# Weight chunks split in halves with the row block outermost, the modulation product in plain fp32 from the raw chunk and placed around the norms, and the small projection first in its layer

## The reference, cut to what matters

```
h = rms_norm(x, norm_w[layer]); proj = h @ w_in[layer]                  # first block, per layer
(a_xbc, a_z, a_dt, b_q, b_k, b_v, b_z, c_q, c_k, c_v, c_f, c_z, gates) = split(proj)
x = x + sum_i(sigmoid(gate_i) * (y_i @ w_proj[layer, i])) @ w_out[layer]

m = silu(cond) @ w_mod[l] + b_mod[l]         # 2 x 1024 @ 1024 x 6144: shift, scale, gate, twice
h = rms_norm(x, norm_mix[l]) * (1 + scale1) + shift1                    # second block, per layer
x = x + gate1 * (merge(attention, pool, fourier of h @ w_in[l]) @ w_out[l])
h = rms_norm(x, norm_ffn[l]) * (1 + scale2) + shift2
x = x + gate2 * ((val * silu(gate)) @ w_down[l])                        # val, gate: conv of h @ w_up[l]
```

## Time and profile before

| | |
|---|---|
| runs | 2406.66, 2407.77, 2414.5 us; median 2407.77 |
| profiled execution | 2407.12 us; span 2405.3 us |
| TensorE busy | 2173.5 us of the span, mean granted clock 0.953 |
| VectorE, ScalarE, GpSimd busy | 1444.4, 1160.4, 697.9 us |
| moved | 330.66 MB, 137 GB/s over the span |

### The profile page before, as it was taken

The page is one execution under the profiler, slowest core; times in us unless marked ns, Lnnn a source line. Parts: engine busy times, 40 slices in busy tenths (PEclk is TensorE's granted clock), DMA queues, the critical chain, the costliest instruction groups (busy, mean ns, idle before and its releaser), DMA issues.

```text
span 2405.3 us, 35434 instructions
## 1 busy us (share of the span) xinstructions
PE 2173.5 (90%) x14868; PEld 1926.8 (80%) x14868; DVE 1444.4 (60%) x1930; ACT 1160.4 (48%) x1688; POOL 697.9 (29%) x208
## 2 busy tenths in 40 slices
PE   5998979997898989996999998989999969998997
PEld 5888879997788889985867776667778858797996
DVE  5677856555676756565267336565554655845675
ACT  4575474544575475544266333444333344645543
POOL 0222333342322423352101132454441112122331
PEclk9999999998899999996999999999999979998999
DMA  5544434545444435552111234334332212253552
GB/s 202 186 164 153 166 106 158 210 176 183 158 159 158 143 120 177 193 193 97 45 45 48 101 114 147 125 140 175 141 140 105 89 56 84 88 193 113 196 182 70
DMA packets 51982, 330.66 MB, mean 137 GB/s; under 512 B 5488, under 2 KB 8688, under 8 KB 14832
## 3 DMA queue, kind: packets, MB, share of 16 engines
q1 hardware_dynamic: 51824, 328.41, 37.9%
HBM read 327.21 MB, written 1.18 MB: 137 GB/s over the span
## 4 chain that ended last, share of the span: by engine, by line
PE 67%; DVE 18%; ACT 11%; issue 3%; POOL 1%; DMA 1%; SPq 0%; ACTq 0%; DVEq 0%
PE ps L731 18%; PE ps L732 18%; PE ps L733 18%; ACT t_hi L1068 5%; DVE t_lo L1378 3%; DVE t_SQA L1388 2%; DVE t_A L1821 2%; PE ps L776 1%; PE ps L744 1%; PE ps L745 1%; PE ps L746 1%; PE ps L777 1%; PE ps L987 1%; PE ps L847 1%; DVE t_A L1806 1%
## 5 line engine op out<-in xcount | busy, mean ns | idle before, releaser
L731 PE MATMUL ps<-t_RB,t_hi 128*128 128x256 f32 (+1 forms) x3712 | 1176.8, 317 | 54.0 <-DVE t_MOD L1431 11.9
L732 PE MATMUL ps<-t_RB,t_hi 128*128 128x256 f32 (+1 forms) x3712 | 1158.2, 312 | 0.0
L733 PE MATMUL ps<-t_RB,t_lo 128*128 128x256 f32 (+1 forms) x3712 | 1156.8, 312 | 0.0
L1847 POOL TENSOR_TENSOR t_lo<-t_raw,t_hi 128x2048 fp32r<-128x2048 f32 (+2 forms) x140 | 619.0, 4424 | 1424.4 <-ACT t_hi L1068 1397.7
L1068 ACT ACTIVATE t_hi<-t_raw 128x2048 fp32r<-128x2048 f32 (+2 forms) x316 | 571.0, 1809 | 769.3 <-PE ps L733 700.4
L731 PEld LDWEIGHTS ps<-t_RB,t_hi 128*128 128x128 f32 x3712 | 720.6, 194 | 125.1 <-issue 22.8
L733 PEld LDWEIGHTS ps<-t_RB,t_lo 128*128 128x128 f32 x3712 | 720.6, 194 | 35.9
L732 PEld LDWEIGHTS ps<-t_RB,t_hi 128*128 128x128 f32 x3712 | 721.3, 194 | 34.6 <-issue 1.2
L1378 DVE TENSOR_TENSOR t_lo<-t_raw,t_hi 128x2048 fp32r<-128x2048 f32 (+2 forms) x176 | 418.3, 2378 | 459.7 <-ACT t_hi L1068 454.1
L1806 DVE SCALAR_TENSOR_TENSOR t_A<-ps,t_V,t_A 128x510 f32<-128x510 f32 (+1 forms) x176 | 102.0, 611 | 119.2 <-ACT t_A L1338 117.6
L744 PE MATMUL ps<-t_hi,t_RB 128*128 128x256 f32 (+1 forms) x320 | 96.5, 302 | 15.8 <-DVE t_RB L1665 10.3
(11 more groups left out here) (304 smaller groups left out, 2205.8 us busy)
## 6 DMA issues: line engine op xcount, KB each, us to landing
t_raw<-in_W SPq DMA_DIRECT2D x286, 1024.0 KB, 4.8
t_raw<-in_W SPq DMA_DIRECT2D x14, 512.0 KB, 3.7
t_A<-cu_scratch SPq DMA_DIRECT2D x8, 512.0 KB, 5.1
t_B<-cu_scratch SPq DMA_DIRECT2D x8, 512.0 KB, 5.8
t_raw<-in_W SPq DMA_DIRECT2D x16, 256.0 KB, 3.0
t_A<-in_C SPq DMA_DIRECT2D x2, 1536.0 KB, 8.2
t_X<-in_X SPq DMA_DIRECT2D x2, 512.0 KB, 4.1
t_X<-in_X SPq DMA_DIRECT2D x1, 1024.0 KB, 7.4
```

The lines of the kernel that those rows point to most:

```text
L731: mm(o, hi[:, k, w], xh(k), start=k == 0, stop=False)
L732: mm(o, hi[:, k, w], xl(k), start=False, stop=False)
L733: i = mm(o, lo[:, k, w], xh(k), start=False, stop=k == nkt - 1)
L1847: tt(t.lo[s][:, 0:w], t.raw[r][:, 0:w], t.hi[s][:, 0:w].bitcast(F), ALU.subtract).then_inc(*up("pool", ("split", u.i)))
```

## The change

1. A chunk wider than 1024 elements is split in two halves of four row blocks. The first half's `lo` is always GpSimd's; the second is GpSimd's for odd chunks where `share` is set, and VectorE's otherwise. `chan` and `toks` take the row block outermost and the column blocks or token blocks inside. The event `used` exists per half. In the list of units GpSimd gets 368 parts and VectorE 138, where they had 140 and 176 splits, most of them twice as wide.
2. The modulation isn't split. `mod` multiplies `raw` in plain fp32 with 32 stationary columns (`C32`, 2 used, the others 0), row block k into the partitions 32 (k mod 4) on: 8 matmuls. ScalarE copies 128 x 256 to `MT`, and `mod2` adds the four partial sums up and turns them by two matmuls with a constant (`sel`), into a bank of the side work's ring. A modulation row holds its `raw` buffer until TensorE has used it.
3. Modulation units come every twelve gemms in block 1 and every three in most of block 2, and `rstd(t, fill)` puts up to two ahead of the sum of squares, one between it and the spreading matmul (now the unit `rstdb`) and one behind: (2, 1, 1) at t = 1, 3 and 4, (2, 1, 0) at t = 2; the last unit stands just ahead of t = 5. So 16 of the 48 units stand at norms and 32 among the gemms.
4. `small(l)` comes first in its layer, with a tick of its own and one empty step ahead of `small4`. `squares(8)` starts after the last `k` gemm.
5. Block 2's attention mask is stored in 768 columns, not 1024.

```diff
 
+    def turn_mod(self):
+
+        if self.open:
+            l, c = self.open
+            self.add("mod2", l=l, c=c, s=(self.sbank(),))
...
@@ -218,30 +227,32 @@
     def some_mods(self, n):
         for _ in range(n):
             if self.mods:
-                l, c = self.mods.pop(0)
-                i = self.chunk("mod", CH, wcols("w_mod_2", l, np.arange(c * 256, c * 256 + 256)))
-                self.split_after(i)
-                self.add("mod", l=l, c=c, i=i, g=(self.bank(),))
-
-                def turned(l=l, c=c):
-                    self.add("mod2", l=l, c=c, g=(self.bank(),))
-                    return
-                    yield
-                self.side.append(turned())
+                self.turn_mod()
+                l, c = self.open = self.mods.pop(0)
+                self.add("mod", l=l, c=c, g=(self.bank(),))
+
+    def need_mods(self, l, j):
+
+        while self.mods and self.mods[0] < (l, 4 * j + 4):
+            self.some_mods(1)
+        if self.open and self.open < (l, 4 * j + 4):
+            self.turn_mod()
 
...
-        i = self.chunk("split", nkt * ncol, fn)
+        i = self.chunk(nkt * ncol, fn)
         nm, per = ncol // 128, 512 // tw
         for m0 in range(0, nm, per):
             last = m0 + per >= nm
             if last and not urgent:
-                self.split_after(i)
+                self.split_after(i, 0)
             n = then(m0) if then else ()
             self.add(kind, l=l, c=c, i=i, g=(self.bank(),), n=n, x=(m0, min(nm, m0 + per), *x))
             if last and urgent:
                 self.drain()
-                self.split_after(i)
+                self.split_after(i, 0)
+            if last:
+                self.split_after(i, 1)
             if self.fine and not last:
                 self.tick()
...
+        self.small(l)
         qk(0)
-        if l == 1:
-            self.side.append(self.squares(8))
-        self.small(l)
         self.vproj(l, "vc", O_VC, 4)
...
+        if l == 1:
+            self.side.append(self.squares(8))
...
+    def rstd(self, t, fill):
+
+        self.some_mods(fill[0])
+        self.add("rstd", l=t, g=(self.bank(),))
+        self.some_mods(fill[1])
+        b = (self.bank(),)
+        self.add("rstdb", l=t, g=b)
+        self.some_mods(fill[2])
+        return b
+
     def plain(self, t):
-        b = (self.bank(), self.bank())
-        self.add("rstd", l=t, g=b)
+        b = self.rstd(t, (2, 1, 0))
...
+    rows = [u for u in units if u.kind == "mod" or u.kind == "split" and u.c == 0]
 
     def load(j):
-        w = widths[j]
+
+        if j >= len(rows):
+            return
+        if j >= NR:
+            old = rows[j - NR]
+            q.wait_ge(at("split", old.i) if old.kind == "split" else at("modmm", old.l, old.c))
+        w = rows[j].x[0]
         e.dma_start(t.raw[j % NR][:, 0:w], t.d["W"][j, :, 0:w]).then_inc(*up(f"w{j % NR}", ("raw", j), by=16))
...
-        if u.kind == "split" and u.i + NR < n:
-            q.wait_ge(at("split", u.i))
-            load(u.i + NR)
+        if u.kind == "mod" or u.kind == "split" and u.x[3]:
+            load(u.x[1] + NR)
...
     def chan(u, nkt, ncol, tw, xh, xl, point, *events):
 
         hi, lo = weights(u, nkt, ncol)
         b = gbank(u)
-        for j, m in enumerate(range(u.x[0], u.x[1])):
-            o, w = b[:, j * tw:(j + 1) * tw], slice(m * 128, m * 128 + 128)
-            for k in range(nkt):
-                q.wait_ge(point(k))
-                mm(o, hi[:, k, w], xh(k), start=k == 0, stop=False)
+        for k in range(nkt):
+            q.wait_ge(point(k), at("split", u.i, k * ncol // 1024))
+            for j, m in enumerate(range(u.x[0], u.x[1])):
+                o, w = b[:, j * tw:(j + 1) * tw], slice(m * 128, m * 128 + 128)
+                mm(o, hi[:, k, w], xh(k), start=k == 0 and j == 0, stop=False)
                 mm(o, hi[:, k, w], xl(k), start=False, stop=False)
-                i = mm(o, lo[:, k, w], xh(k), start=False, stop=k == nkt - 1)
-        i.then_inc(*up("pe", ("mm", u.i, u.x[0]), ("used", u.i), *events))
+                i = mm(o, lo[:, k, w], xh(k), start=False, stop=k == nkt - 1 and m == u.x[1] - 1)
+            taken(u, i, k, nkt, ncol)
+        ended(u, i, nkt * ncol, ("mm", u.i, u.x[0]), *events)
...
     def mod(u):
-        q.wait_ge(at("split", u.i), at("cond"))
-        s = u.i % NS
-        hi, lo = (p[s][:, :].rearrange("p (k c) -> p k c", k=8) for p in (t.hi, t.lo))
+
+        q.wait_ge(at("raw", u.x[1]), at("cond"))
+        w = t.raw[u.x[1] % NR][:, :].rearrange("p (k c) -> p k c", k=8)
         b = gbank(u)
         for k in range(8):
-            c = t.C4[:, k, :, :].rearrange("p q c -> p (q c)")
-            mm(b[0:4, 0:256], c, hi[:, k, :], start=k == 0, stop=False)
-            i = mm(b[0:4, 0:256], c, lo[:, k, :], start=False, stop=k == 7)
-        i.then_inc(*up("pe", ("mm", u.i, 0), ("used", u.i)))
+            j = k % 4
+            i = mm(b[32 * j:32 * j + 32, 0:256], t.C32[:, k, :], w[:, k, :], start=k < 4, stop=k >= 4)
+        i.then_inc(*up("pe", ("modmm", u.l, u.c)))
 
     def mod2(u):
+
         q.wait_ge(at("mt", u.l, u.c))
-        b = gbank(u)
+        b = sbank(u)
         for m in range(2):
-            i = e.transpose(b[:, 4 * m:4 * m + 4], t.MT[:, m * 128:(m + 1) * 128], t.ident[0:4, 0:4])
+            i = mm(b[:, 2 * m:2 * m + 2], t.MT[:, m * 128:(m + 1) * 128], t.vec("sel", 0, 2), start=True, stop=True)
         i.then_inc(*up("pe", ("modt", u.l, u.c), ("mtr", u.l * 24 + u.c)))
...
     def split(u):
-        s, r, w = u.i % NS, u.i % NR, u.x[2]
-        q.wait_ge(at("raw", u.i), was("used", u.i - NS))
-        act(t.hi[s][:, 0:w], t.raw[r][:, 0:w], ACT.Copy).then_inc(*up("act", ("hi", u.i), ("split", u.i)))
+        s, r, w = u.i % NS, u.x[1] % NR, slice(1024 * u.c, min(u.x[0], 1024 * u.c + 1024))
+        q.wait_ge(at("raw", u.x[1]), was("used", u.i - NS, u.c))
+        act(t.hi[s][:, w], t.raw[r][:, w], ACT.Copy).then_inc(
+            *up("act", ("hi", u.i, u.c), ("split", u.i, u.c), ("split", u.i)))
...
-            kind, w, _ = o.chunks[u.i]
-            u.x = ("pool" if kind == "mod" or (u.x[0] and u.i % 5 in (1, 3)) else "dve", kind, w)
+            w, fn = o.chunks[u.i]
+            if u.c == 0:
+                rows.append((w, fn))
+                row[u.i] = len(rows) - 1
+            elif w <= 1024:
+                continue
+            u.x = (w, row[u.i], "pool" if u.c == 0 or u.x[0] and u.i % 2 else "dve", u.c == 1 or w <= 1024)
+        elif u.kind == "mod":
+            u.x = (CH, len(rows))
+            rows.append((CH, wcols("w_mod_2", u.l, np.arange(u.c * 256, u.c * 256 + 256))))
         units.append(u)
-    return units, o.chunks
+    return units, rows
 
 
 def build(nc, units, d):
```

More of the change, by code:

```diff
@@ L526, in whole @@
         for i in range(NS):
-            self.add("split", i=i, x=(False,))
-        self.every = 6
+            for half in range(2):
+                self.add("split", i=i, c=half, x=(False,))
+        self.every = 12
         self.layer1(0)
@@ L1889, in plan @@
     o = Order().whole()
-    units = []
+    units, rows, row = [], [], {}
     for u in o.units:
```

171 lines of the change are left out of this document (92 added, 79 removed).

## The result

| | before | after |
|---|---|---|
| median of the runs, us | 2409.93 (2406.66 to 2414.5, 4 runs) | 2322.97 (2320.64 to 2326.04, 4 runs) |
| profiled execution, us | 2407.12 | 2326.04; span 2324.3, mean granted clock 0.956 |

The ratio is 0.9639, with a 95% interval of 0.9616 to 0.9661: 3.6% faster, 87 us. The forecast was 2332, in a range of 2296 to 2385.

What follows compares the result with a forecast made beforehand. The prediction took TensorE's stream, broken by short chains on other engines, as the bound. Terms -46 + 21.5 - 15 - 17 - 14.5 - 5 = -76 us from 2407.1, plus 0.65 for the median, gave 2332 us, range 2296 to 2385.

Steps and rivals of the forecast that it cites:

- Modulation's matmuls: On TensorE, 48 units costing 100 us become 32 units among the gemms costing 54 us: -46 us.
- the waits that go: TensorE's gemm waits behind `mod2`'s bank (11.9 us) and two short waits for `MT` (3 us) vanish: -15 us.
- The rival with two groups: In modulation units only two column groups share TensorE's time, 0.68 us more for 35 units: 2356 us; chance 10%.
- the one with none: In modulation units column groups don't share at all, 3.76 us per unit, +90: 2422 us, slower than before; chance 5%.
- Norms: Modulation units waiting for rows delay gemms after norms: +11 at t = 1, +2 at t = 2 and 3, +8.5 at t = 4; +21.5 us.
- the loads at the norms cost nothing: Modulation loads at the norms add no delay: 2310 us in total; chance 8%.
- Small projection: Queued one gemm earlier, its turn on TensorE no longer waits in either layer: -17 us.
- Row block outermost: Gemms wait less for their input's last blocks, 2.2 us at three places and 2.9 at three: -14.5 us.
- Halves: Split chunks shorten GpSimd's holds on VectorE, while the earlier half alone gains nothing: -5 us, between -15 and +35.
- GpSimd's holds rule the chains: GpSimd parts in every chunk double two in three TensorE waits inside stages, +30: about 2367 us; chance 12%.
- The modulation's row late among the gemms: Block 1's twelve modulation units each wait 3 us for their row: 2368 us; chance 10%.
- The signs in the profile: Expected afterwards: GpSimd busy some 930 us, VectorE's splits some 180, third and fourth unit waits at t = 1 some 6 and 7.

Runs made afterwards that it cites:

- e2: Changed kernel with all eight matmuls of a modulation unit in one column group instead of four: 2418.88 us, ratio 1.004.
- e1: Changed kernel with no modulation units between a norm's sum of squares and the next gemm, block 1's spacing 9 instead of 12: 2299.23 us, ratio 0.955.
- e9: Changed kernel with halves by the old rule of engines, and both halves' splits placed behind the gemm's last part: 2299.51 us, ratio 0.9545.
- e8: Changed kernel with halves kept, but both halves of a chunk go to the engine the old rule names: 2282.83 us, ratio 0.9478.
- e10: Changed kernel with each GpSimd half done as two instructions of 512 columns, its share of elements the same: 2304.86 us, ratio 0.9569.
- e11: Changed kernel with halves by the old rule of engines and no modulation units behind the norms' sums of squares: 2265.11 us, ratio 0.9403.

## Why the prediction was right, and where it was not

The total was 9 us too high, well inside the range. That it came so near is luck: the four parts were off by 14, 18, 9 and 33 us (the sum as measured, below), two of them too large a gain and two too small.

**Modulation's matmuls (-46) and the waits that go (-15): right.** The modulation alone takes 55.7 us from the stages (2281.7 to 2226.0, the sums of the table's rows), 61 by these terms. The 3 us of short waits for `MT` in them did not go: layer 0 alone has one of 6.5 after (at 219.9 us). The rival with two groups and the one with none are out by e2. A unit is 1.00 us at full clock, and 1.86 just after an idle (542.53 to 544.39, granted clock 0.50), which the forecast's 1.2 had not told apart.

**Norms (+21.5): right mechanism, a third too small.** The norms cost 31.8 us more, 31.5 with the modulation alone. At t = 1 it is 13.3 for the forecast's 11, at t = 2 and 3 6.9 for 2, at t = 4 11.9 for 8.5. The step left out that the unit's copy also stands in ScalarE's queue ahead of the rounding of `h`. It counted the first gemm from the end of the unit's matmuls, and TensorE then idles 1.85 us at t = 1 and 2.44 each at t = 3 and 4. Nor do the units "cost nothing by themselves": the clock is low there, so a unit takes 1.86 us and its `mod2` some 0.9, and over t = 2 and 3 TensorE is busy for 22.2 of 34.4 us where it was for 8.4 of 27.5. e1 shows that the units behind the sums of squares are the cause of all of it but some 5 us (128.3 against 123.6). The rival "the loads at the norms cost nothing" is out.

**Small projection (-17): wrong.** The step "both waits go" held by two thirds of its wait (17.4 to 5.2 us), and the time did not follow: undone, nothing is lost. The step counted a wait that goes as time that is won, without asking what the moved modulation unit and the later squares would meet. Part of it is shown (the unit at 109.92), the whole balance isn't.

**Row block outermost (-14.5): right mechanism, too small.** It is worth 25 us in the changed kernel and 23 beside whole chunks (2384 to 2361). The waits were counted (three times 2.2 and three times 2.9 us, which is 15.3 and not 14.5), the low clock behind them wasn't; it is shown for mixer 1 (3.0 us longer busy, of 7.2). The 6.8 us of layer 0, where the step had nothing, stay open.

**Halves (-5, between -15 and +35): the step that failed most, twice.** It said that "the earlier half by itself gains nothing"; e9 gives it 17 us. And it said that what counts is GpSimd's hold, as busy share times half a length, and that this falls from 0.6 to 0.4 us. Halves by the same rule of engines are worth 78 us, 61 of them beside the early place, and GpSimd's larger share costs 40 back. The average over the kernel hid both: the holds fell by 59 us and rose by 80. So the rival "GpSimd's holds rule the chains", which I gave 12%, was a true mechanism with a price near its own (40 for 35), under a gain that I hadn't seen. What I set against it doesn't come out of the trace: TensorE's waits inside the stages before, without the small projection's, are some 114 us (idle times of 0.15 us and more), not some 45. The Trainium skill (SBUF - State Buffer, SBUF: two separate sides) has the shared port pair as a lock that the loser waits out for a whole instruction. The VectorE split of 3.44 us that is held until GpSimd's ends agrees, and so does it that half the length brought 18 us back. That the other 22 us are holds too isn't shown: with the larger share GpSimd also has more splits queued around its own attention work.

**The modulation's row late among the gemms (10%)**: once, at 109.92, for 6.70 us, and not twelve times. **The signs in the profile**: GpSimd's busy time (961 us for some 930) and VectorE's splits (209 for some 180) came near; the waits ahead of the third and fourth unit at t = 1 are 6.15 and 4.61 us for some 6 and 7.

**The sum as measured.** Modulation alone -25, small projection first +1, row block outermost -23 (2384 to 2361), halves by the old rule of engines -78 (to 2283), GpSimd's larger share +40 (to 2323): -85 for the measured -87. The forecast had -39.5, -17, -14.5 and -5.

**What stays open.** Which piece makes the 61 us: ScalarE's 1.06 us for 1.9, VectorE's 1.3 for 2.3, or GpSimd's 2.5 for 4.6. All three became shorter together in e8, and e10 only shows that the last one counts. And why e11 loses 8 us in layer 0 against e8 and gains 7 in layer 1 wasn't looked into.

## What to carry to other kernels

Cut the bulk work that shares a queue, or a port, with short chains into shorter pieces, and do that before moving work between engines: here halves brought 78 us, and GpSimd's larger share took 40 back, though its 41% busy looked free. Don't put a thing that waits for a transfer behind a chain's first step because TensorE idles there; it holds TensorE's queue, and its follow-up holds another engine's. A wait that is gone is won time only when what stood behind it is looked at too, and a short idle is to be priced with the low clock that follows it.
